# A transformer trunk on one NeuronCore: a longer bridge between two layers, weights split in short pieces, and a last unit of 25 steps

## The reference

```
layer 0:  q,k,v,gates = split(h @ w_in_ab)
          ya = differential attention, 4 heads of 2 x 64 (unit A)
          yb = sliding-window GQA with sinks, 8 heads, chunks of 64, one chunk back (unit B)
          y  = concat(ya * silu(ga), yb * silu(gb)) @ w_out_ab
layer 1:  q,k,v,gate = split(h @ w_in_c)
          yc = chunked attention, 16 heads, 8 chunks back, learned relative bias (unit C)
          y  = (yc * silu(gc)) @ w_out_c
each:     x = x + rms_norm(y, post_norm_g)
```

## Time and profile before

| | us |
|---|---|
| median of 3 runs | 1292.79 (1291.96 to 1293.49) |
| the profiled execution | 1298.37 |
| its span | 1296.5 |
| mean granted TensorE clock | 0.974 |
| PE busy | 1203.4 (93%) |
| DVE busy | 831.2 (64%) |
| ACT busy | 583.8 (45%) |
| POOL busy | 389.9 (30%) |

### The profile page before, as it was taken

The page is one execution under the profiler, slowest core; times in us unless marked ns, Lnnn a source line. Parts: engine busy times, 40 slices in busy tenths (PEclk is TensorE's granted clock), DMA queues, the critical chain, the costliest instruction groups (busy, mean ns, idle before and its releaser), DMA issues. The chain is left out here.

```text
span 1296.5 us, 17416 instructions
## 1 busy us (share of the span) xinstructions
PE 1203.4 (93%) x6480; PEld 1022.5 (79%) x6480; DVE 831.2 (64%) x1730; ACT 583.8 (45%) x1296; POOL 389.9 (30%) x286
## 2 busy tenths in 40 slices
PE   6999999999999988998579999999999999999974
PEld 5978888888887876777467888888888888788753
DVE  5574766757677666675524684857758576585587
ACT  5544443443455546553425453544444444354442
POOL 4323123131344437455351213123131231313212
PEclk9999999999999989998789999999999999999997
DMA  5252111010212213332220212011020210202042
GB/s 200 76 171 61 38 33 44 23 49 17 66 49 66 82 65 114 99 118 92 71 63 20 71 32 69 17 53 49 17 70 17 69 33 17 69 19 68 17 163 98
DMA packets 88451, 83.12 MB, mean 64 GB/s; under 512 B 3216, under 2 KB 76944, under 8 KB 88368
## 3 DMA queue, kind: packets, MB, share of 16 engines
q1 hardware_dynamic: 88368, 82.02, 20.1%
HBM read 73.57 MB, written 13.68 MB: 67 GB/s over the span
## 5 line engine op out<-in xcount | busy, mean ns | idle before, releaser
L1010 PE MATMUL dense<-hT_hi,w_hi 128*128 128x512 f32 x880 | 353.2, 401 | 5.5 <-DVE k_l L1452 5.0
L1010 PE MATMUL dense<-hT_lo,w_hi 128*128 128x512 f32 x880 | 347.3, 395 | 0.0
L1010 PE MATMUL dense<-hT_hi,w_lo 128*128 128x512 f32 x880 | 346.1, 393 | 0.0
L882 POOL TENSOR_SCALAR w_hi<-w_f 128x1024 fp32r<-128x1024 f32 x88 | 94.5, 1074 | 724.5 <-PE dense L1010 623.8
L1254 ACT ACTIVATE e_sb<-e_sb,low 128x256 f32<-128x256 f32 (+7 forms) x256 | 170.3, 665 | 238.1 <-DVE low L1513 237.6
L885 POOL TENSOR_TENSOR w_lo<-w_f,w_hi 128x1024 fp32r<-128x1024 f32 x88 | 216.2, 2457 | 7.3
L1283 ACT ACTIVATE pT_hi<-turned 128x640 fp32r<-128x640 f32 (+3 forms) x224 | 117.2, 523 | 202.4 <-PE pv_ps L1085 115.0
L1010 PEld LDWEIGHTS dense<-hT_hi,w_lo 128*128 128x128 f32 x880 | 167.0, 190 | 37.0
L1010 PEld LDWEIGHTS dense<-hT_hi,w_hi 128*128 128x128 f32 x880 | 167.1, 190 | 32.8 <-issue 6.1
L1010 PEld LDWEIGHTS dense<-hT_lo,w_hi 128*128 128x128 f32 x880 | 167.6, 190 | 25.6
L1577 DVE TENSOR_TENSOR pT_lo<-turned,pT_hi 128x640 fp32r<-128x640 f32 (+3 forms) x224 | 133.7, 597 | 57.6 <-ACT pT_hi L1283 56.7
(11 more groups left out here) (156 smaller groups left out, 1781.6 us busy)
## 6 DMA issues: line engine op xcount, KB each, us to landing
w_f<-in_w_in_c SPq DMA_DIRECT2D x38, 512.0 KB, 4.1
w_f<-in_w_in_ab SPq DMA_DIRECT2D x34, 512.0 KB, 4.1
rel_tiles_dram<-rel_rows_dram SPq DMA_DIRECT2D x1, 5120.0 KB, 22.7
bias<-rel_tiles_dram SPq DMA_DIRECT2D x8, 640.0 KB, 5.3
y<-in_x SPq DMA_DIRECT2D x8, 512.0 KB, 7.7
w_f<-in_w_out_ab SPq DMA_DIRECT2D x8, 512.0 KB, 3.7
x_dram<-y SPq DMA_DIRECT2D x8, 512.0 KB, 5.3
w_f<-in_w_out_c SPq DMA_DIRECT2D x8, 512.0 KB, 3.5
```

Source lines behind the costliest of these rows:

```text
L882: ts(hi, src, 1.0, 1.0, ALU.mult, ALU.mult).then_inc(w_hi_done, 1)
L1010: last = mm(dense[:, x.n % 2, :], lhs[:, d * P:(d + 1) * P], rhs[:, d, x.f * HALF:(x.f + 1) * HALF], start=i == 0, stop=i == 23)
```

## The change

- **Bridge.** BRIDGE is 14, so C0 starts at 158; its extra step is gone, so that each C unit is 20 steps. A new `segment_by` gives the matmuls of nine fills (k, v, g of C0 and v of C1 for half 0, then k, q, v, g of C0 and v of C1 for half 1) step by step: 4 or 5 a step, then 9, then 14 or 15, 12 and 3. Outs of B6 and B7 stand one a step from 145. B7's gates come one step sooner, their lo part in the same step.
- **Norm.** Each row has a table entry of its own (`Row`): steps of the square, of `y * g_post` on DVE (L1748 of the changed kernel), of `y * root + x` on DVE (L1758), of the second square, of the scaling (L1769) and of the transposes. POOL adds nothing any more. x is loaded for four rows at a time into the half of hT_lo that is no longer used, and the scaled row is written there too. The slot of B7's output weights that lay there lies in hT_hi.
- **POOL.** The low part of a weight block is made by four instructions of 256 columns, with one signal after the last.
- **C7.** Gates of the tile pairs but the first come one step sooner, the lo part in the same step, into places of their own (y2_hi, y2_lo); outs of the pairs 2, 3, 0 come two steps sooner. Of C6 only rows 0 and 1 have outs of their own; rows 2 to 7 are added in PSUM ahead of C7's (6 matmuls in a `last_out`). TOTAL is C7's start + 25.

```diff
@@ -76,7 +76,7 @@
 
     def step(self, j):
 
-        return self.start + j + (1 if self.kind == "C" and self.i == 0 and j >= 8 else 0)
+        return self.start + j
 
     def in_tail(self, s):
 
...
@@ -95,12 +95,12 @@
 
 A = [Unit("A", i, 20 * i) for i in range(4)]
 B = [Unit("B", i, 80 + 8 * i) for i in range(8)]
-BRIDGE = 8
-C = [Unit("C", i, 80 + 64 + BRIDGE + 20 * i + min(i, 1)) for i in range(8)]
+BRIDGE = 14
+C = [Unit("C", i, 80 + 64 + BRIDGE + 20 * i) for i in range(8)]
 UNITS = A + B + C
 for n_, u_ in enumerate(UNITS):
     u_.n = n_
-TOTAL = C[7].start + 27
+TOTAL = C[7].start + 25
 
 
 @dataclass(eq=False)
...
@@ -244,10 +245,12 @@
                 if u_.kind == "B" or u_ is C[7]:
                     if h_ == 1:
                         c_ = u_.col(t_ - 1)
-                        GATES.append(Gate(u_, len(GATES), pv_.step + 2, slice(c_, c_ + 2 * P), pv_, len(RECS) - 1))
+                        soon_ = u_ is B[7] or u_ is C[7]
+                        g_ = pv_.step + (1 if soon_ and it_.step > u_.step(3) or u_ is B[7] else 2)
+                        GATES.append(Gate(u_, len(GATES), g_, slice(c_, c_ + 2 * P), pv_, len(RECS) - 1, g_ + (0 if soon_ else 1)))
     if u_.kind == "A" or u_.kind == "C" and u_.i < 7:
         GATES.append(Gate(u_, len(GATES), u_.step(16) + 5, slice(0, SEQ), PVS[-1],
-                          len(RECS) - 1 if u_.deferred else -1))
+                          len(RECS) - 1 if u_.deferred else -1, u_.step(16) + 6))
 
 REC_OF = {}
 for r_, it_, pv_ in RECS:
...
@@ -306,6 +309,20 @@
                 f.step = first + s
 
 
+def segment_by(fills, first, counts):
+    m = 24 * len(FILLS)
+    for b, u, f in fills:
+        FILLS.append(Fill(b, u, f, len(FILLS)))
+    for s, count in enumerate(counts, first):
+        assert s not in PROJ_AT
+        PROJ_AT[s] = (m, m + count)
+        for f in FILLS[-len(fills):]:
+            if m < 24 * (f.n + 1) <= m + count:
+                f.step = s
+        m += count
+    assert m == 24 * len(FILLS)
+
+
 def both(b, u):
     return [(b, u, 0), (b, u, 1)]
 
...
@@ -320,12 +337,9 @@
     gate_, query_ = ("g", B[i_], f_), ("q", B[i_ + 1], B[i_ + 1].half) if i_ < 7 else ("q", C[0], 0)
     segment([query_, gate_] if i_ < 7 else [gate_, query_], B[i_].start, B[i_].start + 7)
 c_ = C[0].start
-segment([("k", C[0], 0), ("v", C[0], 0), ("g", C[0], 0)], c_ - BRIDGE, c_ - 1)
-segment([("v", C[1], 0)], c_, c_ + 3)
-segment([("k", C[0], 1), ("q", C[0], 1)], c_ + 8, c_ + 8)
-segment([("v", C[0], 1)], c_ + 9, c_ + 9)
-segment([("g", C[0], 1)], c_ + 10, c_ + 11)
-segment([("v", C[1], 1)], c_ + 12, c_ + 16)
+segment_by([("k", C[0], 0), ("v", C[0], 0), ("g", C[0], 0), ("v", C[1], 0), ("k", C[0], 1), ("q", C[0], 1),
+            ("v", C[0], 1), ("g", C[0], 1), ("v", C[1], 1)], c_ - BRIDGE,
+           5 * [4] + 4 * [5] + 5 * [9] + [14, 15, 15, 15] + 4 * [12] + 8 * [3])
 for i_ in range(7):
     c_ = C[i_].start
     if 0 < i_ < 6:
...
@@ -379,16 +393,36 @@
     s_ = B[i_ + 1].start + 8
     out_steps((B[i_], B[i_ + 1]), [(s_ + t, 1) for t in (3, 4, 6, 7, 8, 9, 11, 12)])
 s_ = C[0].start
-out_steps((B[6], B[7]), [(s_ - 5, 2), (s_ - 4, 2), (s_ - 1, 2), (s_, 2)])
+out_steps((B[6], B[7]), [(s_ - BRIDGE + 1 + t, 1) for t in range(8)])
 for i_ in range(6):
     out_steps((C[i_],), even_plan(C[i_ + 1].start + 3, 16, 17))
 s_ = C[7].start
-out_steps((C[6],), [(s_ + 4 + t, 1) for t in range(16)], (2, 3, 4, 5, 6, 7, 0, 1))
-NORM = [B[5].start + 1, B[5].start + 4, B[6].start, B[6].start + 5,
-        C[0].start - 3, C[0].start - 2, C[0].start, C[0].start + 1]
-for r_, a_ in enumerate(NORM):
+out_steps((C[6],), [(s_ + 7 + t, 1) for t in range(4)], (0, 1))
+
+
+@dataclass(eq=False)
+class Row:
+    r: int
+    ysq: int
+    yg: int
+    x1: int
+    xsq: int
+    scaled: int
+    turn: int
+
+
+def b_steps(*at):
+    return [B[int(a)].start + round(10 * a) % 10 for a in at]
+
+
+NORM = [Row(0, *b_steps(4.6, 4.7, 5.1, 5.2, 5.4, 5.6)), Row(1, *b_steps(5.1, 5.2, 5.4, 5.5, 5.7, 6.1)),
+        Row(2, *b_steps(5.5, 5.6, 6.0, 6.1, 6.3, 6.5)), Row(3, *b_steps(6.0, 6.1, 6.5, 6.6, 7.0, 7.2))]
+s_ = C[0].start - BRIDGE
+NORM += [Row(r_, *(s_ + a_ for a_ in at_)) for r_, at_ in enumerate(
+    ((3, 4, 5, 5, 6, 9), (5, 6, 7, 7, 8, 10), (7, 8, 9, 9, 10, 11), (9, 10, 11, 11, 12, 13)), 4)]
+for n_ in NORM:
     for half_ in range(2):
-        SPARE_RAW.append((a_ + (5 if r_ < 4 else 6), "turn", (), r_, half_))
+        SPARE_RAW.append((n_.turn, "turn", (), n_.r, half_))
 SPARE_RAW.sort(key=lambda x: x[0])
 SPARES = [Spare(what, step, PRO_USES + n, units, row, half) for n, (step, what, units, row, half) in enumerate(SPARE_RAW)]
 EARLY_AT, LATE_AT = {}, {}
...
@@ -411,7 +445,7 @@
 
 LAST_OUTS, FINAL = [], []
 for k_, p_ in enumerate((1, 2, 3, 0)):
-    s_ = C[7].start + 4 * k_ + 10
+    s_ = C[7].start + 4 * k_ + (8 if k_ else 10)
     for o_ in range(2):
         for half_ in range(2):
             LAST_OUTS.append((s_ + o_, len(LAST_OUTS), 2 * p_ + o_, half_, k_))
...
@@ -882,7 +906,12 @@
             ts(hi, src, 1.0, 1.0, ALU.mult, ALU.mult).then_inc(w_hi_done, 1)
             if new(w_hi_done, n + 1):
                 pool.wait_ge(w_hi_done, n + 1)
-            tt(lo_place(slot), src, hi, ALU.subtract).then_inc(w_ready, 1)
+            lo = lo_place(slot)
+            for h in range(2):
+                for q in range(2):
+                    cols = slice(q * PAIR, (q + 1) * PAIR)
+                    last = tt(lo[:, h, cols], src[:, h, cols], hi[:, h, cols], ALU.subtract)
+            last.then_inc(w_ready, 1)
 
         def alibi(tile, name, n):
             b, width = tile[:, 0, :], tile.shape[2]
...
@@ -1055,8 +1081,15 @@
                 pe.wait_ge(w_ready, PRO_SPLITS + LAST_O.n + 1)
             if new(s_ylo, len(GATES) - 4 + k + 1):
                 pe.wait_ge(s_ylo, len(GATES) - 4 + k + 1)
-            out_matmuls(last_bank(n), [(row * P, hi_place(LAST_O.hi)[:, half, :], lo_place(LAST_O.slot)[:, half, :])])\
-                .then_inc(f_filled, 1)
+            parts = [(y2_hi, y2_lo, row * P, hi_place(LAST_O.hi)[:, half, :], lo_place(LAST_O.slot)[:, half, :])]
+            if row >= 2:
+                if new(w_ready, PRO_SPLITS + LAST_PAIR_O.n + 1):
+                    pe.wait_ge(w_ready, PRO_SPLITS + LAST_PAIR_O.n + 1)
+                if new(s_ylo, len(GATES) - 4):
+                    pe.wait_ge(s_ylo, len(GATES) - 4)
+                w = LAST_PAIR_O
+                parts.insert(0, (yT_hi, yT_lo, row * P, hi_place(w.hi)[:, half, :], lo_place(w.slot)[:, half, :]))
+            out_matmuls(last_bank(n), parts).then_inc(f_filled, 1)
 
         def times_v(p):
             u = p.u
...
@@ -1301,6 +1334,11 @@
             if new(s_y, g.n + 1):
                 act.wait_ge(s_y, g.n + 1)
             older = [x.use for u in UNITS[:g.u.n] for x in OUTS[u] if same_columns(slice(u.col(x.row), u.col(x.row) + P), g.cols)]
+            if g.u is C[7]:
+                if new(s_turn, V_TURNS[-1].idx + 1):
+                    act.wait_ge(s_turn, V_TURNS[-1].idx + 1)
+                copy(y2_hi[:, g.cols], o_sb[:, g.cols], ACT.Copy).then_inc(s_yhi, 1)
+                return
             if older:
                 if new(s_spare, max(older) + 1 - PRO_USES):
                     act.wait_ge(s_spare, max(older) + 1 - PRO_USES)
...
@@ -1686,26 +1733,41 @@
-            for g in GATES_AT.get(s - 1, []):
-                gated_lo(g)
+            for g in GATES:
+                if g.lo == s:
+                    gated_lo(g)
             for _, n, row, half, _ in LAST_AT.get(s - 1, []):
                 last_out(n, row, half)
-            for r in norm_rows(s, 1):
-                if new(n_yr, r + 1):
-                    dve.wait_ge(n_yr, r + 1)
-                if new(s_gpost, 16):
-                    dve.wait_ge(s_gpost, 16)
-                stt(out=y[:, r, :], in0=y[:, r, :], scalar=rowstat[:, 2, r:r + 1], in1=g_post[:], op0=ALU.mult,
-                    op1=ALU.mult).then_inc(n_ys, 1)
-            for r in norm_rows(s, 4):
-                if new(n_xr, r + 1):
-                    dve.wait_ge(n_xr, r + 1)
-                if new(s_gpre, 32):
-                    dve.wait_ge(s_gpre, 32)
-                if new(n_sum, r + 1):
-                    dve.wait_ge(n_sum, r + 1)
-                stt(out=x_place(r), in0=y[:, r, :], scalar=rowstat[:, 5, r:r + 1], in1=g_pre[:], op0=ALU.mult,
-                    op1=ALU.mult).then_inc(n_scaled, 1)
+            for n in NORM:
+                r = n.r
+                if s == n.yg:
+                    if new(n_ysq, r + 1):
+                        dve.wait_ge(n_ysq, r + 1)
+                    if new(s_gpost, 16):
+                        dve.wait_ge(s_gpost, 16)
+                    tt(y[:, r, :], y[:, r, :], g_post[:], ALU.mult).then_inc(n_ys, 1)
+            for n in NORM:
+                r = n.r
+                if s == n.x1:
+                    if new(n_yr, r + 1):
+                        dve.wait_ge(n_yr, r + 1)
```

(6 more changed lines are left out.)

144 lines of the change are left out of this document (77 added, 67 removed).

## The result

The changed kernel takes 1277.80 us (median of 4 runs, 1276.87 to 1278.34) against 1293.14 in the same comparison: a ratio of 0.9873 (95% interval 0.9842 to 0.9905). It is faster by 15.3 us between the medians; 48.5 were forecast. Its profiled execution took 1278.07 us, with a span of 1276.3 and a clock of 0.982. Both profiles hold 6480 matmul and transpose records of TensorE, not the 6450 said ahead.

The account below looks back on a forecast made before the run. TensorE was taken as the bound, losing some 89 us to idling and low clock in three places. Gains 15 + 2.5 + 22 + 9 = 48.5 us gave 1249.9 us profiled, 1244 in the median; range 1228 to 1268.

Parts of the forecast that it names:

- rival (b): Weight splits: GpSimd takes its next piece before a waiting VectorE instruction, so short pieces give nothing; 1257 us, chance 0.06.
- 15 us from B4 to B7: B4 to B7, norm of rows 0 to 3 and short pieces: gain 15 of 22 us, bounds 8 and 20.
- The stop of 2.73 us and its like should go: Norm of rows 0 to 3: TensorE's 2.73 us wait for VectorE's scaled row, and similar ones, vanish with earlier rows.
- 22 us in the bridge: Bridge to layer two and unit C0: gain 22 us of some 41, bounds 12 and 32.
- Step 150's 4.6 us of VectorE: Bridge, step 150: VectorE has 4.6 us of work against TensorE's 2.5, delaying row 7's chain.
- 9 us in the last unit: Last unit, C7: summing twelve of C6's out halves in PSUM and reordering gains 9 us, bounds 3 and 12.
- I add up 6: Last unit: VectorE's time from last pT_lo to last gate's lo falls from 11.4 us to 6.
- 5.5 us: Last unit: about eight y adds leave VectorE in the stretch where it is 86% busy, worth 5.5 us.
- 2.5 us before B4: 22 to 446 us: short pieces give 2.5 us, half of the 5.2 us idle, bounds 0 to 5.
- (a): Bridge: VectorE becomes the bound, so it gives 8 us instead of 22; 1258 us, chance 0.14.
- (c): Weight splits: GpSimd is late, each awaited split costing TensorE up to 1.7 us; with other slower endings, chance 0.06.
- (d): Last unit gives nothing, since VectorE waits for ScalarE and TensorE in line; 1253 us, chance 0.08.

Follow-up runs that it names:

- the pieces alone: Kernel before, with only the low part of a weight made by four instructions of 256 columns; 1289.95 us against 1291.60, ratio 0.9985.
- the narrow sum: Changed kernel, with VectorE's final sum of the first six rows over one column in place of 1024; 1271.52 us, ratio 0.9831.
- the changed kernel with one piece: Changed kernel, with the low part of a weight made in one instruction again; 1283.59 us, ratio 0.9930.
- rows spread ahead of the splits: Changed kernel, steps of rows 0 to 2 moved apart, roots kept before GpSimd's two weight splits of step 126; 1273.12 us, ratio 0.9863.

## Why the prediction was wrong

The sign and the mechanism of the pieces were right, though rival (b) puts them at 13.5 us in all, and they are worth 6.0 to 7.8 in the changed kernel. Three of the four terms were too large. Against the sum 15 + 2.5 + 22 + 9 the stretches give 3.6 + 5.6 + 10.1 + 3.4, less 2.5 in the C units.

- **15 us from B4 to B7: the step "The stop of 2.73 us and its like should go" failed.** I shortened the row's chain and gave it a step more, and took the waits for that chain as all there was. The 3.6 us that came are those of the pieces alone; the moved norm gave none. When the scaled row is early, the second half waits for hT_lo, whose makers stand behind two rows' sums and scalings on VectorE and two rows' squares on ScalarE, in the same step. I had added up VectorE for the bridge but no engine for B5, and ScalarE's squares only in the chain of row 7. The low bound of 8 was no bound either: it counted half the clock as won.
- **22 us in the bridge:** the waits at the transposes were forecast at some 8 us and are 2.5 and 2.4, with smaller ones: right in size. The two largest stops were not in the walk. The first out was moved two steps sooner and I priced only its weights, not the gate it now stands behind (565.62). Step 150's 4.6 us of VectorE I had counted, but set against the transposes; it is the y add at the end of that line that TensorE needed (589.28). "2 for a short fall of the clock" was one fall; there were three, at stops of 3.46, 4.02 and 2.42 us. The low bound is a slip besides: 22 less the 8 us of waits is 14, not 12.
- **9 us in the last unit:** "I add up 6" from the last pT_lo to the last gate's lo is what it is (1256.14 to 1262.13). That is 5.4 us less than before. From C7's first item to the last pT_lo the time grew from 81.2 to 83.2 us, where the 9 us leave a fall of 3.6 (9 less 5.4), which was to come from "5.5 us" of y adds taken off VectorE: this term failed. The outs, two steps sooner, bring rows' adds, product and sum between the last items, which are then late (1243.38 and 1247.90); the narrow sum bears that out in part. Behind the last lo the time stayed 14.2 us.
- **2.5 us before B4** was too small by 3: half of a 5.2 us idle column, when TensorE's busy time in that stretch shrank by 2.4 us as well.
- **Rivals.** (a), VectorE as the bound of the bridge, is nearest to what came, with ScalarE beside it, and VectorE's line stood in the way in B5 and in the last unit too; its 8 us for the bridge were 10. But only three transposes were late by 1.4 us or more, and the two largest stops were at outs, so its sum was met partly by luck. (b) is refuted: with the pieces alone VectorE's instructions on four columns take 0.53 us at most, in the changed kernel with one piece 2.00. (c) is refuted by the absence of any stop on w_lo behind the first 27 us, (d) by the last unit's 3.4 to 5.3 us.
- **Profile and runs.** 20.2 us between the profiles are 15.3 between the medians, since the profiled execution of before was a long one. I subtracted all gains from it as if each of its falls of the clock stood in every run.

What stays open: why the medians give the pieces 1.7 us on the kernel before, when the profiles give 6.7 there and 6.0 in the changed one. Both profiled executions of the kernel before were long, and part of what the pieces take away, such as the stop at 412.65, does not stand in every run at that length; that this makes up the difference is not shown. Open too is which of squares, VectorE's line and the single bank makes the idle time that is left in B5.

## What to carry to other kernels

When a wait is removed, list what else each engine does in that same step, all engines, and ask which of it stands ahead of the next thing TensorE needs; a shorter chain bought nothing here, where two in-order lines stood behind it. A stop that comes of two engines' instructions meeting was 1.55 us in one execution and 4.04 in the next, and a fall of the clock follows only some stops, so cost both with a chance, and take the profiled execution's own distance from the median off first. After moving a step of a table, read each queue it passed: two steps later put a root of 0.7 us behind 6.6 us of subtractions.

## What the runs showed of the hardware

A four-way split of a GpSimd subtraction cost 4 x 782 - 2457 = 671 ns. Where such a subtraction was whole, a VectorE instruction of 0.4 us begun 0.1 us after it took 2.56 us. The same stop, 1.9 to 2.2 us at one out in C6, was followed by a fall of TensorE's clock in some profiles (the change: 67.35 us from C6 to C7, clock 0.97) and by none in others (rows spread ahead of the splits, the same program there: 65.89 us, clock 1.00), a difference of 1.5 us that no edit explains. And in the one profile without VectorE's twelve instructions for rows 0 to 3, the stretch from B4 to B7 had 1.9 us less idle time and 4.9 us less busy time, the latter with the clock at 1.00 in place of 0.94.
